# Two reorderings in the token mixers of a two-layer trunk step: the first decay masks on VectorE, the squares of the A and B heads on ScalarE

## The reference, cut to what matters

```
(a_q, a_k, a_v, b_q, b_k, b_v, c_z, c_xbc, c_dt, d_q, d_k, d_v, gate) = split_proj(proj)
qa = rmsnorm(a_q per head of 64, g_qa)      # likewise ka, qb, kb; qd, kd per head of 32
qa, ka, qb, kb, qd, kd = axial_rope(...)     # latent tokens only
decay  = exp(where(causal, acs[l] - acs[s], -inf))        # branch C, a chunk of 128 tokens
scores = einsum(C, B) * decay;  y_diag = scores @ x        # forward and backward in time
yd = diff_attention(qd, kd_all, vd_all, lam)               # branch D
out = (sum over branches of sigmoid(gate) * (y @ w_br)) @ w_out
```

## Time and profile before

| what | us |
|---|---|
| median of three executions | 1937.18 |
| the three executions | 1935.91, 1937.18, 1944.45 |
| span of the profiled execution | 1943.1 |
| TensorE busy in it | 1833.4 (94%) |
| VectorE, ScalarE busy | 484.2 (25%), 366.2 (19%) |

### The profile page before, as it was taken

How to read it: one execution, slowest core, us unless ns; L and a number is a source line. 1 busy time by engine, 2 the same in 40 slices (tenths; PEclk the granted TensorE clock), 3 DMA queues, 4 the chain that set the end, 5 groups by cost and what they waited for, 6 DMA issues and landing times.

```text
span 1943.1 us, 19460 instructions
## 1 busy us (share of the span) xinstructions
PE 1833.4 (94%) x7728; PEld 814.8 (42%) x7728; DVE 484.2 (25%) x1219; ACT 366.2 (19%) x930; POOL 49.3 (3%) x91
## 2 busy tenths in 40 slices
PE   5999999999999999999889999999998999989987
PEld 3555444444533333433255544444444343324322
DVE  1242322445411101101022523225533111101001
ACT  2131322231500100100023222222214010001000
POOL 2100300000000000000000000000000000000000
PEclk8999999999999999999999899999999999999999
DMA  9265312216599999999964453202257999999997
GB/s 377 89 235 204 121 38 87 109 59 250 177 375 431 426 430 431 429 430 430 427 266 183 171 189 120 87 22 108 93 226 269 376 423 417 430 430 430 430 429 313
DMA packets 66685, 532.90 MB, mean 274 GB/s; under 512 B 6880, under 2 KB 7008, under 8 KB 42816
## 3 DMA queue, kind: packets, MB, share of 16 engines
q1 hardware_dynamic: 63472, 527.59, 66.8%
q0 software_dynamic: 3152, 4.47, 0.7%
HBM read 529.16 MB, written 2.88 MB: 274 GB/s over the span
## 4 chain that ended last, share of the span: by engine, by line
PE 77%; DMA 17%; DVE 3%; ACT 2%; issue 1%; SPq 0%; ACTq 0%; DVEq 0%
PE bank L688 70%; DMA ring<-in_w_e 15%; PE bank_pair L688 4%; PE bank L697 4%; DMA ring<-in_w_ada 1%; DMA ring<-in_w_in 1%; DVE x L2439 0%; DVE scr L2153 0%; ACT xn L1568 0%; ACT xn L1710 0%; DVE scr L2326 0%; ACT scr L1786 0%; DVE scr L2325 0%; ACT scr L1788 0%; DVE xn L2155 0%
## 5 line engine op out<-in xcount | busy, mean ns | idle before, releaser
L688 PE MATMUL bank<-ring,hT 128*128 128x512 f32 (+2 forms) x1376 | 581.4, 575 | 4.5 <-DMA ring<-in_w_in 2.3
L688 PE MATMUL bank<-ring,scr 128*64 128x512 f32 (+1 forms) x2152 | 523.3, 599 | 47.1 <-DMA ring<-in_w_e 36.2
L688 PEld LDWEIGHTS bank<-ring,hT 128*128 128x128 f32 x1376 | 260.2, 195 | 265.9 <-issue 253.2
L688 PE MATMUL bank<-scr 128*64 128x512 f32 (+4 forms) x1612 | 339.1, 545 | 2.2 <-DVE scr L2428 1.1
L688 PEld LDWEIGHTS bank<-ring,scr 128*64 128x64 f32 (+1 forms) x2152 | 173.8, 142 | 365.1 <-issue 293.2
L688 PEld LDWEIGHTS bank<-scr 128*64 128x64 f32 (+3 forms) x1612 | 116.7, 148 | 189.8 <-issue 184.5
L2424 DVE TENSOR_TENSOR scr<-scr,bank 128x512 f32<-128x512 f32 x32 | 22.0, 688 | 458.9 <-PE bank L688 458.9
L1798 ACT ACTIVATE scr<-bank 128x512 f32<-128x512 f32 x32 | 19.1, 597 | 457.9 <-PE bank L688 457.9
L688 PE MATMUL bank_pair<-scr 32*128 32x512 f32 (+6 forms) x352 | 102.1, 501 | 0.0
L697 PEld LDWEIGHTS bank<-cst,scr 128*128 128x128 f32 (+1 forms) x506 | 59.8, 157 | 91.2 <-issue 50.5
L697 PE MATMUL bank<-cst,scr 128*128 128x128 f32 (+1 forms) x506 | 85.2, 289 | 9.1 <-DVE scr L2236 3.3
(11 more groups left out here) (262 smaller groups left out, 1095.4 us busy)
## 6 DMA issues: line engine op xcount, KB each, us to landing
ring<-in_w_e SPq DMA_DIRECT2D x122, 2048.0 KB, 19.4
scr<-in_w_e SPq DMA_DIRECT2D x64, 2048.0 KB, 18.8
ring<-in_w_ada SPq DMA_DIRECT2D x24, 2048.0 KB, 9.5
ring<-in_w_in SPq DMA_DIRECT2D x20, 2048.0 KB, 9.1
ring<-in_w_out SPq DMA_DIRECT2D x4, 2048.0 KB, 8.1
ring<-in_w_in SPq DMA_DIRECT2D x4, 1552.0 KB, 14.6
ring<-in_w_in SPq DMA_DIRECT2D x4, 1536.0 KB, 12.0
ring<-in_w_br SPq DMA_DIRECT2D x4, 1024.0 KB, 4.9
```

The costliest lines, as they stand in the source:

```text
L688: ins = pe.matmul(out, lhsT, rhs, start=start, stop=stop, **kw)
```

## The change

Two edits, each done in both layers.

VectorE: `head_norm` gets an argument `between`, a function called ahead of the rotary of the tiles 1 and 2. For the D heads it is `masked(0)`, which no longer stands behind `head_norm`. So the two mask additions and the two copies of a word now come behind the D heads' gains and ahead of their rotary.

ScalarE: the waits for `d_ready` and for the last unit of A and B, and the first two Squares of the A and B heads, move ahead of the Tanh of `gate0(1)`, behind `root(NT)`. The third Square, with its wait for `sq_free`, moves behind that Tanh and ahead of the copies of `rows(2)`. No instruction is added or taken away, and no wait is dropped; TensorE's, GpSimd's and SyncE's programs stay as they were.

```diff
                 root(NT)
+                act.wait_ge(d_ready, now(d_ready, 1))
+                act.wait_ge(big_act, now(big_act, taken_by(("ab", NT - 1, 1))[1]))
+                for t in range(2):
+                    A(tmp[:, t % 2, :], AB[:, t, :, :]..., ACT.Square).then_inc(act_sq, 1)
                 gate(0, 1)
+                act.wait_ge(sq_free, now(sq_free, NT + 1))
+                A(tmp[:, 0, :], AB[:, 2, :, :]..., ACT.Square).then_inc(act_sq, 1)
                 for h in range(2):
                     rows(2, h)
-                act.wait_ge(d_ready, now(d_ready, 1))
-                act.wait_ge(big_act, now(big_act, taken_by(("ab", NT - 1, 1))[1]))
-                for t in range(NT):
-                    if t >= 2:
-                        act.wait_ge(sq_free, now(sq_free, NT + t - 1))
-                    A(tmp[:, t % 2, :], AB[:, t, :, :]..., ACT.Square).then_inc(act_sq, 1)
...
-            def head_norm(buf, heads, width, per_tile, gq_mul, ready, rotary):
+            def head_norm(buf, heads, width, per_tile, gq_mul, ready, rotary, between=None):
...
                 settle()
+                if between is not None:
+                    between()
                 for t in (1, 2):
                     rotary(t)
...
-                head_norm(dbuf, 16, 32, taken_sq, d_gain, d_ready, turner(...))
...
-                masked(0)
+                head_norm(dbuf, 16, 32, taken_sq, d_gain, d_ready, turner(...),
+                          between=lambda: masked(0))
```

More of the change, by code:

```diff
@@ L1603, in _ @@
                 root(NT)
+                act.wait_ge(d_ready, now(d_ready, 1))
+                act.wait_ge(big_act, now(big_act, taken_by(("ab", NT - 1, 1))[1]))
+                for t in range(2):
+                    A(tmp[:, t % 2, :], AB[:, t, :, :].rearrange("p b n -> p (b n)"), ACT.Square).then_inc(act_sq, 1)
                 gate(0, 1)
+                act.wait_ge(sq_free, now(sq_free, NT + 1))
+                A(tmp[:, 0, :], AB[:, 2, :, :].rearrange("p b n -> p (b n)"), ACT.Square).then_inc(act_sq, 1)
                 for h in range(2):
                     rows(2, h)
-                act.wait_ge(d_ready, now(d_ready, 1))
-                act.wait_ge(big_act, now(big_act, taken_by(("ab", NT - 1, 1))[1]))
-                for t in range(NT):
-                    if t >= 2:
-                        act.wait_ge(sq_free, now(sq_free, NT + t - 1))
-                    A(tmp[:, t % 2, :], AB[:, t, :, :].rearrange("p b n -> p (b n)"), ACT.Square).then_inc(act_sq, 1)
                 for t in range(NT):
@@ L2056, in _ @@
                 dbuf = lambda t: DQ[:, t, :].rearrange("p (h d) -> p h d", h=16)
-                head_norm(dbuf, 16, 32, taken_sq, d_gain, d_ready, turner(dbuf, 16, 32, "cosd", "sind", 2, d_ready))
                 def masked(t):
@@ L2067, in masked @@
                         V.tensor_copy(xmark, dt_[:, 0, 0:1]).then_inc(seg_ready, 1)
-                masked(0)
+                head_norm(dbuf, 16, 32, taken_sq, d_gain, d_ready, turner(dbuf, 16, 32, "cosd", "sind", 2, d_ready),
+                          between=lambda: masked(0))
                 for t in range(NT):
```

## The result

The changed kernel takes 1923.85 us (median of six executions, 1921.28 to 1927.16) beside 1938.93 us for the kernel before (six, 1935.91 to 1944.45). The ratio is 0.9926, with a 95% interval of 0.9912 to 0.9940: 14.3 us less by the ratio, between 11.6 and 17.1. 1918.2 was forecast, in a range from 1912.0 to 1929.4. The profiled execution took 1921.28 us, with a span of 1919.5 in place of the 1943.1 of the forecast's profile.

The account below looks back on a forecast made before the run. TensorE was taken as the bound (77% of the chain, DMA 17%), so its waits and the low clock behind them counted. 2 x (5.6 + 3.9) = 19.0 us off the 1937.2 median gave 1918.2 us, range about 1912 to 1929.4.

Parts of the forecast that it names:

- The order on VectorE: D-head masks ahead of the rotary: two TensorE waits go, a new 0.3 us wait comes; 5.6 us less a layer.
- The first place: TensorE from the first GT product to the third unit of A and B: 11.98 us to become 6.4 a layer.
- The order on ScalarE: Squares moved so the D copy frees its bank before TensorE's transposes need it: 3.9 us less a layer.
- the clock's part: Decays, rows and gate tiles regain full clock once TensorE's waits go: 8.6 us of the 19.0.
- The waits' part: Time back if only TensorE's waits go and the clock still falls: 10.4 us, giving 1926.8 us.
- the second place: TensorE's D transposes and three gate tiles: transposes 4.54 to 2.04 us, tiles 22.38 to 21.0, a layer.
- The low clock behind `columns(3)`: Clock at 0.50 behind sixteen four-column products; taken as unchanged, 1.7 us a layer, 3.4 us kept for the low end.
- The clock falls at both places all the same: Rival: GT, decays and transposes load the array lightly, so the clock stays low; 1926.8 us, chance 0.10.
- Transposes: Rival: only the D transposes let the clock fall, slowing the gate tiles behind them; 1921.0 us, chance 0.10.
- VectorE as the bound: Rival: products with GT come 5.6 us late and TensorE's row waits for the GT bank; 1929.4 us, chance 0.07.
- The DMA: Rival: the mixer ends earlier but waits longer for the experts' weights, hiding the gain; 1937.2 us, chance 0.06.
- ScalarE's new wait: Rival: waiting for `sq_free` ahead of the third Square delays TensorE; 1941.8 us if VectorE's sum comes at 213, chance 0.04.

Follow-up runs that it names:

- the last comparison: Changed kernel again, and with the four-column products spread over the next unit, beside the kernel before (1935.34 us): 1924.85 us (ratio 0.9944) and 1920.85 us (0.9928).
- the second profile of the changed kernel: Profile from running the changed kernel once more, no further edit, against the kernel before: 1924.85 us, ratio 0.9944.

## Why the prediction was right, and where its sum was off

**The order on VectorE** came as worked out. The masks take 1.59 us of the queue (1.58 forecast), the exponentials are over before the unit 1 ends, the waits for L2063 and L1561 are gone, and the new wait is 0.42 us in the first layer (0.3 forecast) and absent in the second. The first place takes 6.46 us where 6.4 was forecast.

**The order on ScalarE** too: two Squares in the idle time, no wait at `sq_free`, no wait at ("ckT"), 1.95 us where 2.04 was forecast, the tiles at 20.87 where 21.0 was.

**The failed term** is the clock's part: "That is 8.6 us of the 19.0." (It is less than half of the sum, not "the larger half" that the forecast calls it.) The waits' part came as forecast: 2 x 2.7 us at the first place (9.15 - 6.46) and 2 x 2.6 at the second (4.54 - 1.95), 10.6 in place of 10.4. The clock's part did not come in full, for two reasons. The 2.9 us a layer behind the first place were read from one execution and counted as if every execution lost them; in 10 layers of five profiles they were lost 3 times, which makes 1.7 us an execution in place of 5.8. And a clock that is kept at a place is not time gained: with the waits left in and the clock kept at both places the time fell by 1.7 us (between 4.7 less and 1.4 more), and with the second place alone kept by nothing (3.3 less to 2.9 more).

The granted clock gives a second estimate. Its mean is 0.98824 over 80 executions of the kernel before and 0.99018 over the 11 of the changed one; at 1.4 us for 0.001 (see the last section) that is 2.7 us, and with the waits 13.3, beside 14.2 measured. In the last comparison, on one chip, it is 0.98973 and 0.99020, 0.7 us, together 11.3; the means there, 1936.2 and 1924.9, differ by 11.3.

Where the rest of the clock's part goes is open, and a sum place by place does not close. The start of branch D fell in 5 of 14 layers without the fall at the second place, but in 0 of the 4 of the changed kernel itself. The low clock behind `columns(3)`, which the forecast took as unchanged, did change: in the 10 layers with the masks behind the rotary and no fill at the first place the unit of A and B behind it took 8.73 to 10.12 us (9.5 in the mean), in the six with the masks ahead and those products together 8.81 or 7.11 (8.0). That speaks for 3 us an execution more, which the forecast did not count. Timeline of TensorE, the second profile of the changed kernel, both layers:

```profile
147.75 7.11 PE L688 MATMUL bank<-ring,hT 128*128 128x512 f32 x16
...
1094.18 8.81 PE L688 MATMUL bank<-ring,hT 128*128 128x512 f32 x16
```

The sign that the forecast's profile was a slow one was there: with the 1.8 us by which a time lies above its span in the changed kernel (1921.28 and 1919.5), that execution took about 1944.9 us, an estimate, 6.2 above the mean of all. The text set the span itself beside the median of times and so found 5.9 where 7.7 is nearer, and took the terms from it all the same. Of the 5.65 us between the forecast and the median, 1.75 are the base: the kernel before has 1938.93 over six executions, and 1937.18 over the three of the forecast.

**The rivals.** "The clock falls at both places all the same" is out: 0 of 20 layers with the changed order at that place. Transposes: sixteen of them in a row at the second place ran at 1.00 (the second stretch of the result), and the tiles behind them took 20.87 us in 10 of 10 layers. The Trainium skill, "TensorE: Matmul & The Clock Gate", section "Part 4: PE-mode transpose", says that the full clock doesn't engage for transposes, which don't count in the same way as work; here they did not bring it down, and the measurement decides. It decides no more than that: these transposes last 1.95 us, and of the two places with waits of some 2 us the one behind transposes fell in 10 of 10 layers, the other in 3 of 10. VectorE as the bound cost 0.42 us in one layer. The DMA did not hide the gain: the waits' part arrives in the time, though the share of DMA in the chain that ended last rose from 17% to 19% of the span. ScalarE's new wait was met before ScalarE came to it.

**What made the range hold** was its high end, 1929.4, which was set by the case with VectorE as the bound and lies above the 1926.8 of the waits alone. The measured 1923.85 lies between 1926.8 and the forecast. The mechanism of the two reorderings was right; that the missing clock stayed inside the range is in part luck, since no case of the forecast had a clock that is kept at both places and still hardly pays.

## What to carry to other kernels

When part of a gain is clock, one profile gives the price of a fall but not how often it happens: take it from several profiles, or from the spread of the executions, before it goes into the sum in full. And a clock kept at one place is a gain only when the median shows it. An instruction that only another engine's next step needs, like a mask ahead of exponentials, can go ahead of a long block on its own queue; the price is the delay of that block's reader, and here that was 0.42 us. Moving work into an engine's idle time is worth checking against the table loads and the waits behind it, in that order.

## What the runs showed of the hardware that was not expected

One program gave times from 1933.9 to 1946.1 us in 46 executions on one chip, and the time goes with the mean granted clock of the execution (0.983 to 0.992): the correlation is -0.90, and 0.001 of clock goes with 1.4 us.

A gap at one and the same place brings the clock down in some executions and not in others: the first place, with 1.9 to 2.4 us of waits in three pieces, in 3 of 10 layers. The second, with 2.25 us in one piece behind transposes, fell in 10 of 10. The Trainium skill, "TensorE: Matmul & The Clock Gate", section "Part 1: The HAM clock gate (the "warmup" mystery)", says that the clock's watch runs free of the kernel, so that the same kernel meets it differently from run to run; the counts of the first place agree.

A clock fall that is kept away at one place can appear at a later one: behind the 1.64 us wait at the start of branch D it was seen only in profiles without the fall at the second place. Why is open; no run here was made for that place alone.
